# A decoder trunk on one core: column sums of five modulation groups as transposes spread over four weight items, and a new order of VectorE's work in the GLA output projection

## The chip, the cores and the metric

The kernel runs on one core of a Trainium2 chip. The metric is the device time of one execution in microseconds (us), lower is better. An execution with the hardware profiler gives the trace that is read here.

## The reference, cut to what matters

One token block of 256 rows (T) by 2048 columns (D) goes through a gated-linear-attention (GLA) layer with a convolutional gated MLP, then a latent-attention (MLA) layer with another MLP. Each block is modulated by vectors computed from a condition vector c:

```python
c_act = jax.nn.silu(c)
mod = c_act @ mod_w[i] + mod_b[i]            # 1 x 2048 times 2048 x 12288
sh_m, sc_m, g_m, sh_f, sc_f, g_f = jnp.split(mod, 6, axis=-1)
h = modulate(rmsnorm(x, norm_mix_g[i]), sh_m, sc_m)
y = gla_mixer(h, ...)                        # its last step: o @ w_o, 256x2048 times 2048x2048
x = x + (1 + g_m)[:, None, :] * y
h = modulate(rmsnorm(x, norm_ffn_g[i]), sh_f, sc_f)
x = x + (1 + g_f)[:, None, :] * conv_ffn(h, ...)
```

## The kernel before, in words

**Weight items.** Every large product streams its weights in items of 128x2048 floats (1 MB; 0.75 MB in the last part of each MLP), 16 to a 2048x2048 matrix. An item passes four stages: SyncE (SP) starts the load into `raw`, ScalarE copies it to a rounded high part (`hi`, L756), VectorE subtracts to get the low part (`lo`, L1202), and TensorE multiplies: 16 matmuls with the high part, then 8 with the low part (L1868, L1869, L1875; in items with transposes between the products L1860 to L1862). There are RAW = 4 slots, so the load of item n waits until TensorE has finished item n-4, and the helpers of ScalarE and VectorE work AHEAD = 3 items before TensorE: at step k of a section VectorE makes the low part of item k+3.

**Modulation groups.** The 14 vectors g = 0 to 13 (2048 wide) are sums of 16 tiles each, `mod_w` rows times a column of c. A modulation step (L1219) is one load of 1 MB into one of MODS = 2 buffers (L550) and one VectorE operation, `acc += mods * c`. Its load waits until the step two before it is done (L548). MOD_PLACES (L437) says at which item's step the modulation steps are done; on SP's queue the load of a step at item k stands right ahead of the load of item k+3 (L626), and on VectorE the step stands ahead of the low part of item k+3.

**Column sums.** When a group is complete, `acc` must be summed over its 128 partitions. For the gates (2, 5, 11, 13) TensorE does four wide products with a matrix of ones (L1940). For shifts and scales it does 16 one-column products with the tile as stationary matrix (L1945) in one block, and one or two tiny VectorE operations finish (`reduced`, L1230): group 3 after item 14 of the section `r`, 6 and 8 after the third item of `up01` and `up02`, 7 and 9 after the third item of `down01` and `down02`.

**GLA output.** Section `r` (16 items) ends with the output of head 3 (`head_out`). Section `gla_out` then multiplies the gated heads by `w_o`. Its left operand is made on the way: TensorE transposes `r_sb` by pairs of tiles (`turn_head`, L1909, 8 fills), ScalarE and VectorE split each fill into `h_hi` (L771) and `h_lo` (L1274, L1281), and the first four items wait for them fill by fill. VectorE's order at the end of `r` and in the first steps (L1577 to L1594, L1339 to L1352):

```python
if k == 15: reduced(3); o_split_lo(0); o_split_lo(1)
mods_at(s.item + k); lo(s.item + AHEAD + k)   # the last: item 2 of gla_out
...
gated_head(3)                                 # then, per step k of gla_out:
if k < 3: o_split_lo(2*k+2); o_split_lo(2*k+3)
if k == 7: add_chunk(1)
mods_at(k); lo(AHEAD + k)
if k in (3, 11): add_chunk(k // 4)            # add_last after the loop
```

`add_chunk` (L1304, L1305) adds a finished chunk of four items to x; `add_last` (L1311 to L1316) adds the last one in two halves, and the norm that follows waits for it.

Of the kernel before, what the change touches and what calls it, by code (L numbers as in the profile page):

```python
# [29 lines left out]
P = 128  # L30
# [19 lines left out]
def sections():  # L50
# [11 lines left out]
        ("r", 1, 16, 4, 0, 0),  # L62
        ("o", 1, 0, 0, 8, 6),
        ("mod_r", 1, 0, 0, 0, 1),
        ("o3", 1, 0, 0, 0, 2),
        ("gla_out", 2, 8, 2, 0, 0),
# [10 lines left out]

    ffn(0, (4, 1, 1), (1, 1, 1))
    s += [
# [58 lines left out]
def yoco_kernel(nc, x, c, positions, mod_w, mod_b, norm_mix_g, norm_ffn_g, gla_w_in, gla_w_gate2,  # L138
# [155 lines left out]

    GATES = (2, 5, 11, 13)

    REDUCE = {0: ("pre", 10), 1: ("pre", 11), 2: ("mod_v", 0), 3: ("mod_r", 0), 4: ("mod_gla", 0),
# [6 lines left out]
    def fills_of(g):  # L304
        return 4 if g in GATES else 1

# [4 lines left out]
    with ExitStack() as ctx:  # L311
# [120 lines left out]
        def taken(m):  # L432
# [6 lines left out]
            ("r", 3, 3, every[:13]), ("r", 4, 0, (13, 13, 14, 15)),  # L439
            ("gla_out", 4, 4, (4, 4, 5, 5, 6, 7, 8, 9, 10, 11, 12, 13)),  # L440
            ("up00", 5, 0, (3, 4, 5, 6, 6, 7) + after_conv[:10]), ("up00", 6, 0, after_conv[10:]),
# [68 lines left out]
        def o_fill(h, t):  # L510
            return (at["o"].ms + 2 * h if h < 3 else at["o3"].ms) + t

# [231 lines left out]
        def _(act):  # L744
# [221 lines left out]
            head_squares(3)  # L966
            hi(s.item + AHEAD + 15)

            def add_section(name, after):

                s = a[name]
                for k in range(16):
                    if k < 3:
                        o_split_hi(2 * k + 2)
                        o_split_hi(2 * k + 3)
# [216 lines left out]
        def _(dve):  # L1192
# [28 lines left out]
            def gate_row(g, j):  # L1221
# [6 lines left out]
                dve.scalar_tensor_tensor(v, ms[:, fill % 2, :], 1.0, v, ALU.add, ALU.add).then_inc(ms_free, 1)  # L1228

            def reduced(g):  # L1230

# [104 lines left out]
            def add_section(name, after):  # L1336

                s = a[name]
                for k in range(15):  # L1339
                    if k < 3:  # L1340
                        o_split_lo(2 * k + 2)
                        o_split_lo(2 * k + 3)
                    if k == 7:
                        add_chunk(s.chunk + 1, 1, slice(W, 2 * W))
                    mods_at(s.item + k)
                    if k < 14:
                        lo(s.item + AHEAD + k)
                    if k in (3, 11):
                        ch = k // 4
                        add_chunk(s.chunk + ch, ch % 2, slice(ch * W, (ch + 1) * W))  # L1350
                add_last(name, after)
                lo(s.item + AHEAD + 14)  # L1352
# [225 lines left out]
            for k in range(16):  # L1578
                score_step(16 + k)
                if 3 <= k < 7:  # L1580
                    gate_row(2, k - 3)
                if k in (8, 11, 14):
                    gated_head((8, 11, 14).index(k))
                if k == 15:
                    reduced(3)
                    o_split_lo(0)
                    o_split_lo(1)
                mods_at(s.item + k)
                lo(s.item + AHEAD + k)
# [45 lines left out]
            def up(layer, g, before=None):  # L1635
# [5 lines left out]
                def body(i, conv_too):  # L1641
                    for k in range(8):
                        mods_at(s.item + 8 * i + k)
# [7 lines left out]
                        if before is not None and not conv_too and k == 2:  # L1651

                            reduced(before)
                        if conv_too and 1 <= k <= 4:
                            conv_lo(i - 1, k - 1, tile_ - 1)
# [5 lines left out]
            def down(layer, g, up_group):  # L1661
# [15 lines left out]
                for k in range(16):  # L1677
# [7 lines left out]
                    if k == 15:  # L1685

                        add_chunk(s.chunk + 3, 1, slice(3 * W, 4 * W))
                    mods_at(s.item + k)
# [4 lines left out]
                    if up_group in GATES:  # L1693

                        if 3 <= k < 7:
                            gate_row(up_group, k - 3)
                        if k == 6:
                            dve.wait_ge(ms_free, reduce_at(up_group) + 4)
                            add_chunk(s.chunk, 0, slice(0, W))
                    elif k == 2 and up_group is not None:  # L1700
                        reduced(up_group)
                    if k % 4 == 3 and k < 15 and not (k == 3 and up_group in GATES):
# [144 lines left out]
        def _(pe):  # L1847
# [84 lines left out]
            def reduce_mod(g, parts=range(4)):  # L1932
# [9 lines left out]
                else:  # L1942
# [4 lines left out]
                    ins.then_inc(ms_done, 1)  # L1947

            def turn_rows(name, fills, tile_of):

# [30 lines left out]
            def section(name, hi_s, lo_s, turned=None):  # L1981
# [198 lines left out]
            for k in range(16):  # L2180
# [11 lines left out]
                if k == 13:  # L2192
                    turn_head(0)
                    turn_head(1)
                if k == 14:
                    reduce_mod(3)
            head_out(3)
# [10 lines left out]
            def ffn(layer, norm, up_groups, down_groups):  # L2208
                for g, blocks in enumerate(UP_BLOCKS):
                    s = a[f"up{layer}{g}"]  # L2210

                    def block_(i, turn):
                        for k in range(8):
# [17 lines left out]
                    for k in range(16):  # L2231
# [7 lines left out]
                        if k < 2:  # L2239
# [3 lines left out]
                            turn_pair(layer, g, blocks - 1, 2 * k + 1)  # L2243
                        if up_groups[g] in GATES:
                            if 2 <= k < 6:
                                reduce_mod(up_groups[g], (k - 2,))
                        elif k == 2 and up_groups[g] is not None:
                            reduce_mod(up_groups[g])

# [169 lines left out]
```

## Time and profile before

| | |
|---|---|
| median of 3 runs | 2425.52 us (2422.24 to 2425.59) |
| the profiled execution | 2417.79 us, of which its span 2416.0 us |
| granted TensorE clock, mean | 0.981 |
| busy: TensorE, VectorE, ScalarE, GpSimd | 96%, 76%, 45%, 5% of the span |
| one-column products L1945 | 128 products in 8 blocks |
| section gla_out, items 0 to 15 | 434.40 to 533.83 us |

In timelines a row gives start and duration in us, engine, line, operation, `out<-in` and tile; the bracket is the idle time just before and what ended it. Matmul rows overlap: what a matmul costs is the distance to the next start, not its duration.

### The profile page before, as it was taken

What the parts mean: (1) busy time and instruction counts of PE and PEld (TensorE: products, weight loads), DVE (VectorE), ACT (ScalarE), POOL (GpSimd) and SP (SyncE); (2) the same over time, 40 slices, a digit from 0 to 9 for tenths busy, and PEclk for the clock granted to TensorE, in tenths of its full rate; (3) what the DMA queues carried; (4) which work ended last, traced back from release to release, by engine and by line L of the source; (5) the groups of instructions that cost most, each with busy time, mean ns of one, the idle gap of its engine ahead of it and who ended that gap; (6) DMA issues with size and microseconds to landing.
All of it is one profiled execution on the core that took longest, in us unless ns stands there. A gap on an engine that the chain in (4) does not pass through costs nothing.

```text
span 2416.0 us, 26990 instructions
## 1 busy us (share of the span) xinstructions
PE 2326.8 (96%) x10880; PEld 1883.1 (78%) x10880; DVE 1835.2 (76%) x1728; ACT 1097.7 (45%) x1192; POOL 126.8 (5%) x145
## 2 busy tenths in 40 slices
PE   5999999989999999999999999999999999999998
PEld 2478887778887888888877788777887888878876
DVE  5868997787998888888888777787786555654565
ACT  2244434344544345533454555434654345543553
POOL 0022730000000000000000000000000000000000
PEclk8999999999999999999999999999999999999999
DMA  9958689587987988789878465785775555555544
GB/s 362 378 199 300 248 313 355 203 316 274 346 326 274 367 312 308 279 334 363 306 253 326 131 223 196 271 320 211 277 283 203 191 188 180 189 174 192 188 164 152
DMA packets 259808, 632.91 MB, mean 262 GB/s; under 512 B 23505, under 2 KB 32745, under 8 KB 233978
## 3 DMA queue, kind: packets, MB, share of 16 engines
q1 hardware_dynamic: 258050, 625.90, 72.6%
q10 hardware_dynamic: 1656, 5.60, 0.6%
q8 instruction: 70, 1.15, 0.2%
q14 instruction: 32, 0.26, 0.0%
HBM read 629.36 MB, written 2.10 MB: 261 GB/s over the span
## 4 chain that ended last, share of the span: by engine, by line
PE 81%; DVE 8%; DMA 5%; ACT 3%; issue 2%; SPq 1%; POOL 1%; DVEq 0%; POOLq 0%; ACTq 0%
PE gm L1868 22%; PE gm L1869 22%; PE gm L1875 21%; PE tp L1909 2%; DMA raw<-in_ffn_w_down_dram 2%; PE gm L1860 2%; PE gm L1862 2%; PE gm L1861 2%; DVE w_lo L1202 2%; ACT w_hi L756 2%; DVE acc L1219 1%; DVE conv L1609 1%; DMA raw<-in_gla_w_o_dram 1%; PE ms L2007 1%; DMA mods<-in_mod_w_dram 1%
## 5 line engine op out<-in xcount | busy, mean ns | idle before, releaser
L1202 DVE TENSOR_TENSOR w_lo<-raw,w_hi 128x2048 fp32r<-128x2048 f32 (+1 forms) x378 | 851.8, 2256 | 350.5 <-ACT w_hi L756 349.0
L756 ACT ACTIVATE w_hi<-raw 128x2048 fp32r<-128x2048 f32 (+1 forms) x378 | 703.9, 1863 | 709.0 <-DMA raw<-in_ffn_w_up_dram 240.0
L1868 PE MATMUL gm<-w_hi,h_hi 128*128 128x512 f32 x1816 | 722.0, 398 | 1.9 <-DVE h_lo L1281 1.6
L1869 PE MATMUL gm<-w_hi,h_lo 128*128 128x512 f32 x1816 | 709.7, 391 | 0.0
L1875 PE MATMUL gm<-w_lo,h_hi 128*128 128x512 f32 x1816 | 448.8, 389 | 0.0
L1219 DVE SCALAR_TENSOR_TENSOR acc<-mods,c_col,acc 128x2048 f32<-128x2048 f32 x180 | 423.0, 2350 | 6.2 <-DMA mods<-in_mod_w_dram 5.8
L1868 PEld LDWEIGHTS gm<-w_hi,h_hi 128*128 128x128 f32 x1816 | 342.3, 189 | 80.4 <-issue 6.3
L1869 PEld LDWEIGHTS gm<-w_hi,h_lo 128*128 128x128 f32 x1816 | 342.4, 189 | 70.3 <-issue 1.7
L1875 PEld LDWEIGHTS gm<-w_lo,h_hi 128*128 128x128 f32 x1816 | 340.8, 188 | 71.0 <-DVE w_lo L1202 0.2
L1868 PE MATMUL gm<-w_hi,a_hi 128*128 128x512 f32 x692 | 279.6, 404 | 10.8 <-DVE a_lo L1632 8.8
L1869 PE MATMUL gm<-w_hi,a_lo 128*128 128x512 f32 x692 | 274.7, 397 | 0.0
L1609 DVE SCALAR_TENSOR_TENSOR conv<-tp,cv_col,conv 128x255 f32<-128x255 f32 (+1 forms) x352 | 152.4, 478 | 86.2 <-ACT conv L1018 82.8
L1875 PE MATMUL gm<-w_lo,a_hi 128*128 128x512 f32 x692 | 172.2, 389 | 0.0
L1868 PEld LDWEIGHTS gm<-w_hi,a_hi 128*128 128x128 f32 x692 | 133.3, 193 | 44.3 <-DVE a_lo L1632 11.9
L1869 PEld LDWEIGHTS gm<-w_hi,a_lo 128*128 128x128 f32 x692 | 133.3, 193 | 28.9 <-issue 1.4
L1875 PEld LDWEIGHTS gm<-w_lo,a_hi 128*128 128x128 f32 x692 | 129.9, 188 | 27.0
L762 ACT ACTIVATE u<-gm 128x1024 f32<-128x1024 f32 x76 | 77.5, 1020 | 147.0 <-PE gm L1875 142.8
L1018 ACT ACTIVATE conv<-tp,cv_col 128x256 f32<-128x256 f32 x176 | 88.3, 560 | 117.4 <-PE tp L1909 116.9
L694 POOL TENSOR_TENSOR sq<-sq 128x2 f32<-128x2 f32 x4 | 4.9, 1220 | 1856.1 <-ACT tp L788 1856.1
L725 POOL TENSOR_TENSOR ex<-ex,qk_t 128x512 f32<-128x512 f32 x32 | 78.8, 2480 | 105.3 <-ACT ex L929 105.3
L771 ACT ACTIVATE h_hi<-tp,ab 128x256 fp32r<-128x256 f32 x64 | 32.0, 563 | 84.2 <-DVE ab L1402 47.8
L1860 PE MATMUL gm<-w_hi,h_hi 128*128 128x512 f32 x136 | 58.1, 427 | 8.7 <-DVE h_lo L1281 5.3
(261 smaller groups left out, 2129.7 us busy)
## 6 DMA issues: line engine op xcount, KB each, us to landing
raw<-in_ffn_w_up_dram SPq DMA_DIRECT2D x176, 1024.0 KB, 5.1
mods<-in_mod_w_dram SPq DMA_DIRECT2D x170, 1024.0 KB, 7.1
raw<-in_ffn_w_down_dram SPq DMA_DIRECT2D x64, 1024.0 KB, 5.1
raw<-in_gla_w_in_dram SPq DMA_DIRECT2D x48, 1024.0 KB, 5.2
mods<-in_kv_mod_w_dram SPq DMA_DIRECT2D x32, 1024.0 KB, 6.9
raw<-in_ffn_w_down_dram SPq DMA_DIRECT2D x32, 768.0 KB, 4.4
raw<-in_gla_w_o_dram SPq DMA_DIRECT2D x16, 1024.0 KB, 7.4
raw<-in_mla_w_o_dram SPq DMA_DIRECT2D x16, 1024.0 KB, 5.3
```

The lines of the kernel that those rows point to most:

```text
L725: pool.tensor_tensor(f, f, s, ALU.mult).then_inc(xq_made, 1)
L756: act.activation(w_hi[:, k % RAW, 0:words], raw[:, k % RAW, 0:words], ACT.Copy).then_inc(hi_made, 1)
L762: act.activation(dst, gm[:, par] if src is None else src, func).then_inc(u_made, 1)
L1018: ins = act.activation(conv[:, j % 2, side, :], tp[:, bank, side * T:(side + 1) * T], ACT.Identity, scale=cv_col[:, layer, 2, cs], bias=cv ...
L1202: dve.tensor_tensor(w_lo[:, k % RAW, 0:words], raw[:, k % RAW, 0:words], w_hi[:, k % RAW, 0:words].bitcast(F32), ALU.subtract).then_inc(lo ...
L1219: return dve.scalar_tensor_tensor(total, tile_, ck, total, ALU.mult, ALU.add)
L1609: ins = dve.scalar_tensor_tensor(v, tp[:, bank, side * T:(side + 1) * T - shift], cv_col[:, layer, tap, cs], v, ALU.mult, ALU.add)
L1860: pe.matmul(o, hi_s[:, kt, tok], wh[:, j, :], start=kt == 0, stop=False)
L1861: pe.matmul(o, hi_s[:, kt, tok], wl[:, j, :], start=False, stop=False)
L1868: pe.matmul(o, hi_s[:, kt, tok], wh[:, j, :], start=kt == 0, stop=False)
L1869: pe.matmul(o, lo_s[:, kt, tok], wh[:, j, :], start=False, stop=False)
L1875: return pe.matmul(o, hi_s[:, kt, tok], wl[:, j, :], start=False, stop=kt == total - 1)
```

## The change

Groups 3, 6, 7, 8 and 9 (TURNED) get four fills in place of one: after each of four consecutive items TensorE does four transposes of `acc` into a bank of `ms`, and VectorE sums each bank along its rows (`row_sums`, 128x512 to 128x4), then adds the bias. Group 3 moves from the end of `r` to the steps after items 4 to 7 of `gla_out`. In the MLPs this work, and that of the gates, stands ahead of the modulation steps and the low part of its step. In `gla_out` VectorE does four low splits ahead of `gated_head(3)`, the low part of an item ahead of the modulation steps and adds of its step, and the modulation step of `r`'s last item comes after the low part of item 3. One modulation step moves from item 5 to item 4 and one from 4 to 3. ScalarE does the high splits of a pair ahead of the high part of the item.

```diff
-        ("o", 1, 0, 0, 8, 6), ("mod_r", 1, 0, 0, 0, 1), ("o3", 1, 0, 0, 0, 2),
+        ("o", 1, 0, 0, 8, 8), ("mod_r", 1, 0, 0, 0, 4),
...
-    ffn(0, (4, 1, 1), (1, 1, 1))
+    ffn(0, (4, 4, 4), (4, 4, 1))
...
+    TURNED = (3, 6, 7, 8, 9)
...
-            ("gla_out", 4, 4, (4, 4, 5, 5, 6, 7, 8, 9, 10, 11, 12, 13)),
+            ("gla_out", 4, 4, (3, 4, 4, 5, 6, 7, 8, 9, 10, 11, 12, 13)),
...   ScalarE, end of r
-            hi(s.item + AHEAD + 15)
+            for k in range(3):
+                o_split_hi(2 * k + 2)
+                o_split_hi(2 * k + 3)
+                hi(s.item + AHEAD + 15 + k)
...   VectorE
+            def row_sums(g, j):
+                fill = reduce_at(g) + j
+                dve.wait_ge(ms_done, made(fill))
+                dve.reduce_sum(modc[:, 1, 4 * j:4 * j + 4],
+                               ms[:, fill % 2, :].rearrange("p (b k) -> p b k", b=4), AX_X).then_inc(ms_free, 1)
...   VectorE, add_section of gla_out
-                for k in range(15):
-                    if k < 3:
-                        o_split_lo(2 * k + 2)
-                        o_split_lo(2 * k + 3)
-                    if k == 7:
-                        add_chunk(s.chunk + 1, 1, slice(W, 2 * W))
-                    mods_at(s.item + k)
+                for k in range(2, 15):
+                    if 5 <= k < 9:
+                        row_step(3, k - 2)
                     if k < 14:
                         lo(s.item + AHEAD + k)
-                    if k in (3, 11):
+                    if k in (3, 7, 11):
                         ch = k // 4
                         add_chunk(s.chunk + ch, ch % 2, slice(ch * W, (ch + 1) * W))
+                    mods_at(s.item + k)
...   VectorE, end of r
-                if k == 15:
-                    reduced(3)
-                    o_split_lo(0)
-                    o_split_lo(1)
-                mods_at(s.item + k)
-                lo(s.item + AHEAD + k)
+                if k < 15:
+                    mods_at(s.item + k)
+                    lo(s.item + AHEAD + k)
...
+            for f in range(4):
+                o_split_lo(f)
             gated_head(3)
+            lo(s.item + AHEAD + 15)
+            o_split_lo(4)
+            o_split_lo(5)
+            lo(s.item + AHEAD + 16)
+            mods_at(s.item + 15)
+            o_split_lo(6)
+            o_split_lo(7)
+            lo(s.item + AHEAD + 17)
...   TensorE
+            def reduce_turned(g, part):
+                pe.wait_ge(mod_used, KT * (g - 1))
+                fill = reduce_at(g) + part
+                o = ms_open(fill)
+                for b in range(4):
+                    c0 = part * W + b * P
+                    ins = pe.transpose(o[:, b * P:(b + 1) * P], acc[:, g % 2, c0:c0 + P], ident[:, :])
+                ins.then_inc(ms_done, 1)
...   TensorE, first body of gla_out
+                        if turned and k >= 4:
+                            reduce_turned(3, k - 4)
...   TensorE, up and down
-                            if g and not turn and k == 2 and down_groups[g - 1] is not None:
-                                reduce_mod(down_groups[g - 1])
+                            if g and not turn and 2 <= k < 6 and down_groups[g - 1] is not None:
+                                reduce_turned(down_groups[g - 1], k - 2)
```

## Rows read from the trace of the kernel before

**Rows 1.** The page: busy time and share of the span of each engine

```profile
PE 2326.8 (96%) x10880; PEld 1883.1 (78%) x10880; DVE 1835.2 (76%) x1728; ACT 1097.7 (45%) x1192; POOL 126.8 (5%) x145
```

**Rows 2.** Windows: us, busy PE, PEld, DVE, ACT, POOL, granted clock, DMA share, GB/s

```profile
434.00:484.00 50.00, 47.23 (x218) 38.32 (x217) 40.05 (x38) 20.36 (x26) 3.31 (x2) 1.00 0.61 230
484.00:534.00 50.00, 46.50 (x195) 36.98 (x195) 44.31 (x23) 23.17 (x25) 2.20 (x2) 0.97 0.93 355
1287.00:1330.00 43.00, 37.25 (x164) 29.68 (x162) 37.47 (x25) 18.82 (x22) 1.27 (x2) 0.96 0.93 350
```

**Rows 3.** Timeline of TensorE: end of `r`, item 4 and item 15 of gla_out

```profile
420.75 3.70 PE L1945 MATMUL ms<-ones,acc 128*128 128x1 f32 x32 [0.36 <-DVE r_sb L1571]
424.32 0.48 PE L1868 MATMUL gm<-w_hi,h_hi 128*128 128x512 f32 x1
...
461.80 0.39 PE L1868 MATMUL gm<-w_hi,h_hi 128*128 128x512 f32 x1
462.03 0.39 PE L1869 MATMUL gm<-w_hi,h_lo 128*128 128x512 f32 x1
...
526.61 0.50 PE L1860 MATMUL gm<-w_hi,h_hi 128*128 128x512 f32 x1 [3.43 <-DVE w_lo L1202]
```

**Rows 4.** Timeline of TensorE: between 435.61 and 436.51 four transposes; a wait at 443

```profile
435.61 0.39 PE L1862 MATMUL gm<-w_hi,h_lo 128*128 128x512 f32 x1
...
436.20 0.48 PE L1860 MATMUL gm<-w_hi,h_hi 128*128 128x512 f32 x1
436.51 0.40 PE L1861 MATMUL gm<-w_lo,h_hi 128*128 128x512 f32 x1
...
443.45 0.47 PE L1860 MATMUL gm<-w_hi,h_hi 128*128 128x512 f32 x1 [2.40 <-DVE h_lo L1281]
```

**Rows 5.** Groups by shape: the one-column products, and a read of one bank of `ms`

```profile
L1945 PE MATMUL ms<-ones,acc 128*128 128x1 f32 x256 | 29.4, 249 | 0.4 <-DVE r_sb L1571 0.4
...
L1228 DVE SCALAR_TENSOR_TENSOR gate_b<-ms,gate_b 128x512 f32<-128x512 f32 x16 | 11.0, 685 | 0.0
```

**Rows 6.** Windows of 10 us from a block's start (groups 3, 6, 8), and one with transposes

```profile
420.70:430.70 10.00, 9.95 (x53) 8.69 (x54) 5.11 (x4) 1.59 (x1) 0.00 (x0) 0.83 0.36 125
840.20:850.20 10.00, 10.00 (x61) 8.85 (x61) 8.55 (x5) 2.55 (x2) 0.00 (x0) 1.00 1.01 390
...
1118.60:1128.60 10.00, 10.00 (x55) 8.83 (x54) 8.64 (x5) 2.67 (x3) 0.00 (x0) 0.83 1.03 392
...
589.00:601.00 12.00, 12.00 (x56) 9.93 (x55) 7.82 (x4) 4.65 (x4) 0.00 (x0) 1.00 0.91 337
```

**Rows 7.** Timeline of VectorE: steps 3 to 5 of gla_out, and the last add

```profile
464.86 2.29 DVE L1202 TENSOR_TENSOR w_lo<-raw,w_hi 128x2048 fp32r<-128x2048 f32 x1 [4.67 <-ACT w_hi L756]
467.07 1.22 DVE L1304 TENSOR_TENSOR u<-u,gate_b 128x1024 f32<-128x1024 f32 x1
...
469.47 4.80 DVE L1219 SCALAR_TENSOR_TENSOR acc<-mods,c_col,acc 128x2048 f32<-128x2048 f32 x2
474.18 2.29 DVE L1202 TENSOR_TENSOR w_lo<-raw,w_hi 128x2048 fp32r<-128x2048 f32 x1
...
531.03 0.69 DVE L1311 TENSOR_TENSOR u<-gm,gate_b 128x512 f32<-128x512 f32 x1
```

**Rows 8.** Timeline of SP's queue: a modulation step's load, then that of item 12

```profile
496.52 0.33 SPq L550 DMA_DIRECT2D mods<-in_mod_w_dram  x1
496.90 0.43 SPq L540 DMA_DIRECT2D raw<-in_gla_w_o_dram  x1
```

**Rows 9.** Timeline of ScalarE: the high parts of items 8 and 12

```profile
481.88 1.92 ACT L756 ACTIVATE w_hi<-raw 128x2048 fp32r<-128x2048 f32 x1 [9.47 <-DMA raw<-in_gla_w_o_dram]
...
504.03 1.92 ACT L756 ACTIVATE w_hi<-raw 128x2048 fp32r<-128x2048 f32 x1 [3.40 <-DMA raw<-in_gla_w_o_dram]
```

**Rows 10.** The page's DMA issues: KB each, median us from issue to landing

```profile
raw<-in_gla_w_in_dram SPq DMA_DIRECT2D x48, 1024.0 KB, 5.2
```

**Rows 11.** DMA issues between 484 and 534 us, same columns

```profile
raw<-in_gla_w_o_dram SPq DMA_DIRECT2D x5, 1024.0 KB, 9.6
```

More of the change, by code:

```diff
@@ L62, in sections @@
         ("r", 1, 16, 4, 0, 0),
-        ("o", 1, 0, 0, 8, 6),
-        ("mod_r", 1, 0, 0, 0, 1),
-        ("o3", 1, 0, 0, 0, 2),
+        ("o", 1, 0, 0, 8, 8),
+        ("mod_r", 1, 0, 0, 0, 4),
         ("gla_out", 2, 8, 2, 0, 0),
@@ L304, in fills_of @@
     def fills_of(g):
-        return 4 if g in GATES else 1
+        return 4 if g in GATES or g in TURNED else 1
     def reduce_at(g):
@@ L510, in o_fill @@
         def o_fill(h, t):
-            return (at["o"].ms + 2 * h if h < 3 else at["o3"].ms) + t
+            return at["o"].ms + 2 * h + t
         UNIT_STEP = (0, 1) + tuple(n + 1 for n in range(2, len(UNITS)))
@@ L966, in _ @@
             head_squares(3)
-            hi(s.item + AHEAD + 15)
+            for k in range(3):
+                o_split_hi(2 * k + 2)
+                o_split_hi(2 * k + 3)
+                hi(s.item + AHEAD + 15 + k)
             def add_section(name, after):
                 s = a[name]
-                for k in range(16):
-                    if k < 3:
-                        o_split_hi(2 * k + 2)
-                        o_split_hi(2 * k + 3)
+                for k in range(2, 16):
                     if k % 4 == 3 and k < 15:
@@ L1228, in gate_row, with turned_columns, row_step @@
                 dve.scalar_tensor_tensor(v, ms[:, fill % 2, :], 1.0, v, ALU.add, ALU.add).then_inc(ms_free, 1)
+            def row_sums(g, j):
[3 more added lines that the diff above has]
+                               ms[:, fill % 2, :].rearrange("p (b k) -> p b k", b=4), AX_X).then_inc(ms_free, 1)
+            def turned_columns(g):
+                dve.wait_ge(ms_free, reduce_at(g) + 4)
+                tile_, col = mod_bias(g)
+                bias = pcol[:, tile_, col:col + KT]
+                if g in SHIFT:
+                    step.link(dve.tensor_tensor(ab[:, A_OF[SHIFT[g][0]] + 1, :], modc[:, 1, :], bias, ALU.add))
+                else:
+                    norm, gain = SCALE[g]
+                    step.link(dve.tensor_tensor(modc[:, 0, :], modc[:, 1, :], bias, ALU.add))
+                    dve.scalar_tensor_tensor(ab[:, A_OF[norm], :], modc[:, 0, :], 1.0,
+                                             pcol[:, 0, gain:gain + KT], ALU.add,
+                                             ALU.mult).then_inc(columns_on, 1)
+                    dve.wait_ge(columns_on, list(SCALE).index(g) + 1)
+            def row_step(g, k):
+                if 3 <= k < 7:
+                    if g in GATES:
+                        gate_row(g, k - 3)
+                    else:
+                        row_sums(g, k - 3)
+                if k == 6:
+                    if g in GATES:
+                        dve.wait_ge(ms_free, reduce_at(g) + 4)
+                    else:
+                        turned_columns(g)
             def reduced(g):
@@ L1338, in add_section @@
                 s = a[name]
-                for k in range(15):
-                    if k < 3:
-                        o_split_lo(2 * k + 2)
-                        o_split_lo(2 * k + 3)
-                    if k == 7:
-                        add_chunk(s.chunk + 1, 1, slice(W, 2 * W))
-                    mods_at(s.item + k)
+                for k in range(2, 15):
+                    if 5 <= k < 9:
+                        row_step(3, k - 2)
                     if k < 14:
                         lo(s.item + AHEAD + k)
-                    if k in (3, 11):
+                    if k in (3, 7, 11):
                         ch = k // 4
                         add_chunk(s.chunk + ch, ch % 2, slice(ch * W, (ch + 1) * W))
+                    mods_at(s.item + k)
                 add_last(name, after)
@@ L1642, in body @@
                     for k in range(8):
+                        if before is not None and not conv_too:
+                            row_step(before, k)
                         mods_at(s.item + 8 * i + k)
@@ L1650, in body @@
                             lo(s.item + AHEAD + 8 * i + k)
-                        if before is not None and not conv_too and k == 2:
-                            reduced(before)
                         if conv_too and 1 <= k <= 4:
@@ L1687, in down @@
                         add_chunk(s.chunk + 3, 1, slice(3 * W, 4 * W))
+                    if up_group is not None:
+                        row_step(up_group, k)
                     mods_at(s.item + k)
@@ L1692, in down @@
                         last_tiles(0)
[L1693 to L1701, printed above, removed]
+                    if up_group in GATES and k == 6:
+                        add_chunk(s.chunk, 0, slice(0, W))
                     if k % 4 == 3 and k < 15 and not (k == 3 and up_group in GATES):
@@ L2194, in _ @@
                     turn_head(1)
-                if k == 14:
-                    reduce_mod(3)
             head_out(3)
@@ L2243, in ffn @@
                             turn_pair(layer, g, blocks - 1, 2 * k + 1)
-                        if up_groups[g] in GATES:
-                            if 2 <= k < 6:
+                        if up_groups[g] is not None and 2 <= k < 6:
+                            if up_groups[g] in GATES:
                                 reduce_mod(up_groups[g], (k - 2,))
-                        elif k == 2 and up_groups[g] is not None:
-                            reduce_mod(up_groups[g])
+                            else:
+                                reduce_turned(up_groups[g], k - 2)
             ffn(0, "norm1", (5, 7, 9), (6, 8, 10))
```

## The prediction

> **What bounds the kernel now.** I read the page first: TensorE is busy 96% of the span [rows 1], so time saved on TensorE counts wherever nothing else sets the pace, and anything that makes it wait costs. Then I read the windows, because that share is an average. In the first half of the GLA output section the transfer engines are busy 0.61 of the time, in the second 0.93 at 355 GB/s, with VectorE busy 44.3 of 50 us [rows 2]. An item costs TensorE 24 products at a pitch of 0.23 [rows 3], 5.4 us, and in the second half every item comes with one modulation step, so 2 MB must land in that time: TensorE lives there from hand to mouth. The timelines confirm it. The high part of item 8 is only started at 481.88 [rows 9], although TensorE had reached item 4 at 461.80 and needs item 8 four items later, at about 483.6; the section ends with a wait of 3.43 for the last low part [rows 3]. Two more things show ahead of that section: a block of one-column products of 3.57 (420.75 to 424.32) after a wait of 0.36 [rows 3], and a wait of 2.40 for `h_lo` [rows 4].
>
> **Part 1, the column sums in the MLPs (groups 6 to 9).** Eight blocks take 29.4 us busy together, 3.7 each; the start-to-start distance of group 3's is 3.57 [rows 3, 5], and I take 3.6. Four transposes between products: from 435.61 to 436.51 is 0.90, less two pitches of 0.23 is 0.44 [rows 4], so four groups cost 1.8. Saved 1.8 per group, 7.2 for four. The clock adds to it: in the 10 us from group 8's block the mean granted clock is 0.83, so TensorE stood at 1.2 GHz for a third of it; four such windows stand at 0.83, those of groups 3, 7, 8 and 9 (two are shown), and only group 6's at 1.00 [rows 6]. At most 10 x 0.17 = 1.7 is lost in each; part of the low stretch lies on the block itself, so I take 1.4. If nothing fell any more, that is 4.2 for three groups; the bounds are 0 and 5.1. A stretch with four transposes between items, as the change makes them, stands at 1.00 [rows 6]. VectorE gets four sums of 128x512 per group. The nearest row reads such a bank in 0.685 [rows 5]; 2.7 us per group, spread over four steps. At group 6 VectorE is busy 8.55 of 10 [rows 6], one step of 5.4 becomes 0.7 longer, and its parts are made three items ahead: I cost it at nothing. In `down02` it is not free: VectorE is busy 37.5 of 43 [rows 2] and the last items are starved, so 1.0 of the gain goes back there (bounds 0 and 2.7). The sums and gate rows now ahead of the low part wait for TensorE's fill one item back, which is done when VectorE, three items ahead in the weights but held by their loads, gets there; nothing. The loads at groups 6 and 8 run at 390 GB/s: 2.1 MB in 5.4 us, just TensorE's pace, so the gain stays. Part 1: 7.2 + 4.2 - 1.0 = 10.4, in round numbers **10.5 us faster** (6 to 13).
>
> **Part 2, the start of the GLA output.** The block goes (3.57 + 0.36), with it the low clock behind it (0.83 [rows 6], 1.7 us). The wait of 2.40 goes as well: the splits of fills 2 and 3 no longer stand behind a modulation step, a low part and the gating of head 3. What is late next: the splits of fills 6 and 7, which now stand behind the modulation step of `r`'s last item (2.35, as one in rows 7). I take 1.3 of it, bounds 0 and 2.35. So item 4 starts 3.57 + 0.36 + 1.7 + 2.4 - 1.3 = 6.7 earlier, at 455.1. The four transposes cost 1.8 afterwards.
>
> **Part 3, low parts ahead of modulation steps: the decisive one.** The load of the step at k goes to SP right ahead of the load of item k+3 and waits until the step two before it has been done. Before, VectorE did that step ahead of the low part of item k+1; so a load hung on the low part three items back. Now the step stands behind the low part of its row, and a load hangs on the low part **two** items back. One turn of that ring: from the issue of item 12's load (496.90) to its high part (504.03) 7.1 [rows 8, 9], high part 1.9, low part 2.2, modulation step 2.35 [rows 7], and 0.4 from the step's issue to the item's (496.52 to 496.90) [rows 8]. That is 14.0 for two items, 7.0 each, against TensorE's 5.4; by three items, as before, it was 4.7 and hidden. In steps 3, 7 and 11 an add of 2.4 (467.07 to 469.47 [rows 7]) now stands in the ring too.
>
> Laid out: item 3 ends at 455.1; the low part of item 6 starts 3.06 later (461.80 to 464.86 [rows 3, 7]) and ends at 460.4, the add at 462.8, the first step at 465.2. Only then can SP issue the third step and item 7 (465.6); it lands at 472.7, its low part ends at 476.9, the second step at 479.2, and item 8 goes out at 479.6. Its high part ends at 488.6 instead of 483.8 [rows 9]. Then every 14.0, with an add twice: item 10 at 493.6, 12 at 510.0, 14 at 524.0, 16 (the first of `up00`) at 540.4. Item 16 lands at 547.5, its low part ends at 551.7, and the last modulation step at 554.1. Behind them in VectorE's order stands the first half of the last add, at 531.03 before [rows 7], and behind that the norm and all that follows. **23 us later**, with Part 2 and the 1.8 inside, since all of it lies before the ring. The row sums of group 3 stand in the ring's steps 5 to 8 and make TensorE wait for a bank at items 6 and 7, where it would wait for weights anyway: nothing more. The wait itself will drop the clock; that falls into waiting time as well.
>
> The one price that is uncertain is the landing. Alone it is 5.2 [rows 10], in the saturated stretch 9.6 [rows 11]; the ring runs the transfer engines at three quarters, one step and one item at a time, which is item 12's case (7.1). Five turns are priced with it: 23 - 5 x 1.9 = 13.5 at the low end, 23 + 5 x 2.5 = 35.5 at the high end, where the high end would need full transfer engines and so is hardly reached.
>
> **Sum.** Against the profiled execution, 2417.8: + 23 - 10.5 = 2430.3. It stands 7.7 below the median of the runs, 2425.5; on that the forecast is **2438.0 us**, 12.5 slower (0.5%). A measurement of this kernel can tell some 0.2%, 4.9 us, from no change.
>
> **Rivals.**
> - **The ring doesn't bind (faster).** The saturated stretch before was paced by the transfer engines (0.93 busy, 9.6 to land), not by order; were VectorE far enough ahead for the new order to cost only waiting that is there anyway, the section would keep Part 2's 6.7, less 1.8, and get back some 2 of the 3.4 at item 15: 7, with Part 1's 10.5 together 17.5, 2408. Against: the low part can't be done before its item lands, and VectorE waited 4.67 for one already at step 3 [rows 7]. Chance 0.17.
> - **Short landings (no change).** With the transfer engines free between turns an item lands near 5.2, and the ring costs 13.5: + 3, 2428.5. For: the engines idle a quarter. Against: two transfers go out together each time. With what lies around it chance 0.12.
> - **Transposes don't hold the clock (slower still).** TensorE's clock would fall after each group of four, and the 4.2 of Part 1 would not come: 2442. Chance 0.10. The Trainium skill, TensorE: Matmul & The Clock Gate, Part 4: PE-mode transpose, says that a transpose doesn't count as work for the clock; by that rule alone groups of transposes would lower it. The trace disagrees where they stand between items, at 1.00 [rows 6].
> - The forecast itself: 0.61, own range 2429 to 2450.
>
> The change does more than its name says: five groups are turned, not one. Left out of it, Part 1 would be nothing and the time 2448; it is in the diff, so I give that no chance.
>
> **Chances and range.** Faster by over 0.2%: 0.17, the first rival. Within: 0.12. Slower: 0.61 + 0.10 = 0.71. The range 2416 to 2451 takes in the forecast with its landing bounds, the second and third rival and the near side of the first; left out are most of the 0.17 below and a little above.
>
> **What would show it.** Right: the high part of `gla_out`'s item 8 ends near 488.6 and the last add's first half starts near 554; TensorE waits 3 to 9 us several times between items 7 and 15; the loads L550 in that section wait for L1219, and the transfer engines stand near 0.75; TensorE reaches item 4 at 455; L1945 shrinks to three blocks (3, 6, 7, 8, 9 gone); no low clock at 1026, 1118 and 1261. Wrong: items at 5.5 us through the section; or a low clock still behind the transposes; or the row sums near 1.4 us each, which would starve `down02`.

## The result and the profile after

The changed kernel takes 2438.6 us (median of six runs, 2435.35 to 2445.4), the kernel before in the same comparison 2425.56 (six runs, 2422.24 to 2427.34): 1.006 times as long, with a 95% interval from 1.0043 to 1.0076. It is slower, by 13.0 us between the medians (14.6 by the ratio) where 12.5 were forecast. The profiled execution of after has a span of 2435.0 us at a mean granted clock of 0.978.

The page's busy times, then the windows that answer to [rows 2] with one more between them (columns as there):

```profile
PE 2320.7 (95%) x10800; PEld 1877.1 (77%) x10800; DVE 1847.2 (76%) x1748; ACT 1098.2 (45%) x1192; POOL 125.0 (5%) x145
```

```profile
434.00:484.00 50.00, 39.06 (x180) 31.55 (x180) 34.73 (x30) 16.15 (x17) 0.00 (x0) 0.93 0.48 173
484.00:534.00 50.00, 42.88 (x174) 34.27 (x173) 32.48 (x19) 17.68 (x17) 0.00 (x0) 0.93 0.79 295
534.00:560.00 26.00, 17.92 (x73) 14.99 (x71) 19.89 (x13) 10.21 (x12) 5.25 (x5) 0.79 0.63 232
1287.00:1330.00 43.00, 42.34 (x187) 33.77 (x185) 36.02 (x25) 16.40 (x19) 0.00 (x0) 1.00 0.94 346
```

TensorE's busy total hardly moved, and that alone would hide the matter. Both windows of the GLA output show it: TensorE is busy 39.1 and 42.9 us of 50 where it was 47.2 and 46.5 [rows 2], and in the second one VectorE fell from 44.3 to 32.5 us and the transfer engines from 0.93 to 0.79. All three have room, and none of them is full: that is what a ring of waits looks like. SyncE's queue shows who holds it. Its waits from 430 to 560 us (in total, times, longest) in after:

```profile
SPq L550 <- DVE acc L1219: 83.3, 10, 15.7
SPq L540 <- PE gm L1895: 28.1, 4, 8.9
```

In before the loads of the items (L540) mostly wait for TensorE to free a slot, and the loads of the steps (L550) wait little more than half as long (in total, times, longest):

```profile
SPq L540 <- PE gm L1862: 62.1, 7, 18.0
SPq L550 <- DVE acc L1219: 46.5, 10, 9.4
SPq L540 <- PE gm L1875: 17.0, 3, 10.9
```

The queue's timeline in after. The rows of L540 are the loads of items 7, 8, 10, 12, 14 and 16:

```profile
465.56 0.43 SPq L540 DMA_DIRECT2D raw<-in_gla_w_o_dram  x1
479.18 0.33 SPq L550 DMA_DIRECT2D mods<-in_mod_w_dram  x1
479.55 0.43 SPq L540 DMA_DIRECT2D raw<-in_gla_w_o_dram  x1
...
493.64 0.43 SPq L540 DMA_DIRECT2D raw<-in_gla_w_o_dram  x1
...
510.14 0.43 SPq L540 DMA_DIRECT2D raw<-in_gla_w_o_dram  x1
...
524.16 0.43 SPq L540 DMA_DIRECT2D raw<-in_gla_w_o_dram  x1
...
540.53 1.86 SPq L540 DMA_DIRECT2D raw<-in_ffn_w_up_dram  x3
```

And one turn as VectorE sees it (timeline; the bracket is the wait ahead): a low part, two modulation steps and a row sum, then nothing to do for 6.48 us, the next low part.

```profile
474.59 2.29 DVE L1202 TENSOR_TENSOR w_lo<-raw,w_hi 128x2048 fp32r<-128x2048 f32 x1 [9.45 <-ACT w_hi L756]
476.80 4.80 DVE L1219 SCALAR_TENSOR_TENSOR acc<-mods,c_col,acc 128x2048 f32<-128x2048 f32 x2
481.52 0.68 DVE L1234 TENSOR_REDUCE modc<-ms 128x4 f32<-128x512 f32 x1
488.69 2.29 DVE L1202 TENSOR_TENSOR w_lo<-raw,w_hi 128x2048 fp32r<-128x2048 f32 x1 [6.48 <-ACT w_hi L756]
```

TensorE's waits in the section, in order of time:

```profile
482.35 1.09 PE L1989 MATMUL ms<-ident,acc 128*128 128x128 f32 x4 [9.77 <-DVE modc L1234]
...
493.99 0.63 PE L1989 MATMUL ms<-ident,acc 128*128 128x128 f32 x4 [3.04 <-DVE modc L1234]
...
519.32 0.47 PE L1901 MATMUL gm<-w_hi,h_hi 128*128 128x512 f32 x1 [1.33 <-ACT w_hi L756]
...
533.20 0.50 PE L1901 MATMUL gm<-w_hi,h_hi 128*128 128x512 f32 x1 [2.74 <-ACT w_hi L756]
...
542.38 0.80 PE L1893 MATMUL gm<-w_hi,h_hi 128*128 128x512 f32 x1 [3.43 <-DVE w_lo L1202]
...
554.35 1.86 PE L1978 MATMUL ms<-ones,acc 128*128 128x1 f32 x8 [4.65 <-DVE acc L1219]
...
566.22 0.79 PE L1893 MATMUL gm<-w_hi,h_hi 128*128 128x512 f32 x1 [1.35 <-DVE h_lo L1316]
```

The row at 554.35 is the block of group 4, which waits for the last modulation step. The last row is the first item of `up00`. In the trace of before it stands 22.9 us earlier:

```profile
543.32 0.80 PE L1860 MATMUL gm<-w_hi,h_hi 128*128 128x512 f32 x1 [1.36 <-DVE h_lo L1281]
```

### The profile page after: what moved, and what is told of

The parts are those of the page before. It is cut to its first block, busy times and chain, and to the rows that moved or that the text cites. A ratio compares the mean times of both kernels' runs of the same rounds, so it can differ in the third digit from the quotient of the medians.

```text
span 2435.0 us, 26862 instructions
## 1 busy us (share of the span) xinstructions
PE 2320.7 (95%) x10800; PEld 1877.1 (77%) x10800; DVE 1847.2 (76%) x1748; ACT 1098.2 (45%) x1192; POOL 125.0 (5%) x145
## 4 chain that ended last, share of the span: by engine, by line
PE 78%; DVE 9%; DMA 6%; ACT 3%; issue 2%; SPq 1%; POOL 0%; DVEq 0%; POOLq 0%; ACTq 0%
PE gm L1901 21%; PE gm L1902 21%; PE gm L1908 21%; PE tp L1942 2%; DMA raw<-in_ffn_w_down_dram 2%; ACT w_hi L756 2%; DVE w_lo L1202 2%; DVE acc L1219 2%; PE gm L1893 2%; PE gm L1895 2%; PE gm L1894 2%; DVE conv L1648 1%; DMA raw<-in_gla_w_o_dram 1%; PE ms L2052 1%; PE ms L2186 1%
## 5 line engine op out<-in xcount | busy, mean ns | idle before, releaser
L1219 DVE SCALAR_TENSOR_TENSOR acc<-mods,c_col,acc 128x2048 f32<-128x2048 f32 x180 | 422.6, 2348 | 7.0 <-DMA mods<-in_mod_w_dram 5.9
```

What stands on the lines that cost most here:

```text
L1219: return dve.scalar_tensor_tensor(total, tile_, ck, total, ALU.mult, ALU.add)
```

## The experiments

Each kernel was timed in turn with the kernel before on one chip; ratios are to that. The sets ran on three chips, so kernels of different sets are compared by their ratios. The first four share one set of runs of before (median 2423.66 of 17), the next four another (2425.5 of 17), the last two a third (2423.82 of 7).

**1. After, with the modulation steps ahead of the low part again.**

```diff
     in add_section of gla_out, for k in range(2, 15):
+                    mods_at(s.item + k)
                     if k < 14:
                         lo(s.item + AHEAD + k)
...
-                    mods_at(s.item + k)
```

> The changed kernel with one edit: in the GLA output section VectorE does the modulation steps of a step ahead of its low part again; all else stays. The ring theory: a load hangs on the low part three items back again, 4.7 us per item, so the transfers (some 5.4 per item and step) set the pace. Item 8's load goes out near 465 to 466 instead of 479.6, that of item 16 near 511 instead of 540.5, the wait of TensorE for a bank of the row sums is gone or under 2 us, and the section gives back some 30 us or more: 2404 to 2410, 15 to 21 below the kernel before. Rival, the row sums of group 3 are what stops TensorE (it waits 9.8 and 3.0 for them in the trace of the changed kernel): they stay where they are, so the time stays within 5 us of the changed kernel's 2438.6.

Measured: 2402.32 us (2399.48 to 2406.2), ratio 0.9911 [0.989, 0.9932]. One line moved back, past the low part and in steps 3, 7 and 11 past the add, turns 13 us slower into 21 us faster, a little more than was expected. SyncE issues item 7 at 458.99, item 8 at 466.27 and item 16 at 508.08, where after had 465.56, 479.55 and 540.53:

```profile
458.99 0.43 SPq L540 DMA_DIRECT2D raw<-in_gla_w_o_dram  x1
...
466.27 0.66 SPq L540 DMA_DIRECT2D raw<-in_gla_w_o_dram  x1
...
508.08 4.69 SPq L540 DMA_DIRECT2D raw<-in_ffn_w_up_dram  x2
```

The transposes of group 3 stand in the same four places and now wait for nothing, and the wait for the last low part is down to 0.27.

**2. After, with only SyncE's order changed:** in `gla_out` the load of an item goes out ahead of the load of the modulation step. VectorE's order is that of after.

```diff
-                for m in mod_at.get(n - AHEAD, ()):
+                late = a["gla_out"].item <= n - AHEAD < a["gla_out"].item + 16
+                for m in () if late else mod_at.get(n - AHEAD, ()):
                     load_mod(*m)
...
                 load_item(n, src)
+                for m in mod_at.get(n - AHEAD, ()) if late else ():
+                    load_mod(*m)
```

> The changed kernel with one edit: in the GLA output section SP issues the load of an item ahead of the modulation load of its step, where the changed kernel has it behind; VectorE's new order stays. The ring theory says that the new order costs only because an item's load stands behind a modulation load that waits for a step; with the queue turned an item's load hangs on the step one further back, so again three items, and it lands some 2.5 earlier: 2404 to 2412, close to the kernel with the old order. Rival, the new order is bad in itself (VectorE waits with the low part for the high part and does its steps too late, so the steps pile up): then this kernel stays near 2438.6, at least 2430.

Measured: 2404.84 us (2401.11 to 2407.41), ratio 0.9922 [0.9901, 0.9943], on a par with the first. The ring needs both of its halves: VectorE's step behind a low part that waits for its load, and a load behind the load of a step. Breaking either frees the section; so what cost the time was neither the order on VectorE nor the order on SyncE, but the two together.

**3. Before, with only the new order of low part, adds and modulation steps.** No group is turned, no split is dealt early.

```diff
     in add_section of gla_out, for k in range(15):
-                    if k == 7:
-                        add_chunk(s.chunk + 1, 1, slice(W, 2 * W))
-                    mods_at(s.item + k)
                     if k < 14:
                         lo(s.item + AHEAD + k)
-                    if k in (3, 11):
+                    if k in (3, 7, 11):
                         ...
+                    mods_at(s.item + k)
```

> The kernel before with one edit: in the GLA output section the low part, and the add, stand ahead of the modulation steps of their step; no transposed sums, no other order at the end of r. The ring theory: the ring of two items holds from item 8 to item 16, four turns of 14 with the adds of steps 3, 7 and 11 in it, so item 8's load near 478, item 12's near 515, item 16's near 546, and the norm some 30 later: 2448 to 2460, slower than both kernels. Rival, the loss in the changed kernel comes from its early start meeting loads that can't follow, or from the row sums: then this one costs under 10 us, 2426 to 2435.

Measured: 2454.84 us (2450.24 to 2458.23), ratio 1.0127 [1.0104, 1.015], 31 us slower than before. This prices the ring alone. The loads of items 8, 12 and 16 went out at 486.93, 522.70 and 553.34, 7 to 9 us later than expected; 5.2 of it is TensorE reaching `gla_out` later than in before's trace (439.56 against 434.40). In its windows the transfer engines drop to 0.41 and 0.70 and TensorE's clock to 0.84 in the second:

```profile
434.00:484.00 50.00, 47.45 (x208) 37.60 (x207) 34.16 (x36) 20.52 (x28) 3.31 (x2) 0.97 0.41 148
484.00:534.00 50.00, 35.75 (x130) 27.89 (x129) 27.55 (x14) 12.92 (x14) 0.00 (x0) 0.84 0.70 261
```

**4. Before, with only groups 6 to 9 turned,** and the order of the GLA output as it was (TURNED = (6, 7, 8, 9); group 3 stays a block at the end of `r`; the gate rows of the MLPs stand where the change has them).

> The kernel before with the transposed sums of groups 6 to 9 alone (and the gate rows where the change has them); the GLA output as before. By the prediction's first part 10.5 us faster, 2415. By what the trace of the changed kernel shows, less: group 7's block hid a wait for a_lo that now shows with 2.3, and down02 takes its gain back, so 5 to 8 us: 2417.5 to 2420.5. Rival, that the transposes and row sums bring nothing in the whole (the clock falls at another place instead, supply bound stretches absorb the rest): 2423 to 2428.

Measured: 2417.5 us (2413.43 to 2423.31, 12 runs), ratio 0.9977 [0.9963, 0.9991]: 5.6 us faster by the ratio, 2 to 9 by its interval. Less than the 10.5 of Part 1; where it went is in the section on the prediction.

**5 and 6. Parts of the first experiment undone:** group 7 alone as a block again, then groups 6 to 9 all as blocks (TURNED = (3, 6, 8, 9), and TURNED = (3,)).

> The kernel of e1_mods_first with group 7 alone summed by the block of one-column products again, after item 2 of down01. Theory: that block (3.6) hid a wait of item 3 for a_lo, which ends some 2.9 after item 2, and with the transposes 2.3 of it shows as a wait; so turning group 7 gained 0.8 plus at most 1.4 of clock, not 3.2. Here TensorE shows no wait for a_lo at item 3, and the stretch from item 2's start to item 6's start of down01 is 0.8 longer (27.1 against 26.3 in the changed kernel) if the clock falls behind the block as in the kernel before, and shorter than there if it doesn't. The whole time stays within 2 us of e1_mods_first's 2402. Rival, the prediction's price: the stretch grows by 3.2 and the time by 3.

> The kernel of e1_mods_first with groups 6 to 9 summed by blocks of one-column products again: the early start of the GLA output and the turned group 3 alone. If the parts add up, it lies 21.3 less 6.2 = 15 below the kernel before (e1_mods_first less what e4_turned gained alone): 2408 to 2410. Of these, 7 to 8 come from the section up to item 4 and the end of it as the schedule had it, the rest from item 15's wait and the norm. Rival, the MLP part gains more when the trunk arrives earlier, or its low clocks fall elsewhere: 2412 or more, or under 2404.

Measured: 2402.45 us (2397.8 to 2407.88), ratio 0.9906 [0.988, 0.9932] for the fifth, and 2410.78 (2406.47 to 2414.83), 0.9943 [0.9924, 0.9963] for the sixth. Turning group 7 back changes nothing in the time that these runs can tell. TensorE shows no wait for `a_lo` there, as expected, but the stretch from item 2 to item 6 of `down01` takes 28.69 where 27.1 was expected, with a granted clock of 0.66 in the 10 us from the block's start. The sixth against before is the GLA output without the ring: 13.8 us faster (0.0057 x 2425.5); with the four groups' 5.6 that is 19.4, and the first experiment gave 0.0089 x 2424 = 21.6. The two parts add, within the intervals.

**7. The first, with two modulation steps one item earlier.**

```diff
-            ("gla_out", 4, 4, (3, 4, 4, 5, 6, 7, 8, 9, 10, 11, 12, 13)),
+            ("gla_out", 4, 4, (2, 3, 4, 5, 6, 7, 8, 9, 10, 11, 12, 13)),
```

> The kernel of e1_mods_first with the modulation steps of the GLA output at items 2, 3, 4, ... 13, one each, in place of 3, 4, 4, 5, ... 13: the first load goes out one item earlier and no step is doubled. By the ring by three, item 8 and the last low part come 1 to 2 earlier and the time is 1 to 3 below e1_mods_first: 2399 to 2402. Rival, from item 8 on the transfer engines set the pace and the end of the section is TensorE's own in e1_mods_first (its wait at item 15 is down to 0.27), so that nothing is left to gain: within 1 us of it.

Measured: 2401.07 us (2398.03 to 2401.96), ratio 0.9899 [0.9877, 0.9921]. The gain over the first, 1.2 us by the medians and 2.9 by the ratios, is inside the intervals.

**8. The first, with the row sums and gate rows of the MLPs behind the low part of their step,** as one would place work that nobody seems to wait for.

```diff
-                        if before is not None and not conv_too:
-                            row_step(before, k)
                         ...   the low part
+                        if before is not None and not conv_too:
+                            row_step(before, k)
     the same for row_step(up_group, k)
```

> The kernel of e1_mods_first with the row sums and gate rows of the MLPs behind the low part of their step, where the gate rows stood before. Theory: VectorE is three items ahead there and the sums cost nothing in either place but for down02, where the loads are late at the end: 0 to 1 faster, 2401 to 2403. Rival, that the sums ahead of the low part hold up the chain of loads and steps in down02 (its items start 1.6 later at item 14 in the changed kernel than its item 4 would allow): 2 to 3 faster, below 2400.

Measured: 2413.82 us (2409.14 to 2421.95, 12 runs), ratio 0.9954 [0.994, 0.9969]: 10.4 slower than the first by the ratios, 11.5 by the medians, where I had expected no loss. A miss, and the most useful one. `ms` has two banks: the transposes of the third step need the bank that the row sum of the first gives back. TensorE's waits for a row sum between 800 and 1330 us, and one of them in the timelines of TensorE and VectorE:

```profile
PE ms L1989 <- DVE modc L1234: 10.4, 5, 3.8
```

```profile
847.99 1.09 PE L1989 MATMUL ms<-ident,acc 128*128 128x128 f32 x4 [3.82 <-DVE modc L1234]
```

```profile
844.95 2.29 DVE L1202 TENSOR_TENSOR w_lo<-raw,w_hi 128x2048 fp32r<-128x2048 f32 x1 [0.91 <-ACT w_hi L756]
847.15 0.68 DVE L1234 TENSOR_REDUCE modc<-ms 128x4 f32<-128x512 f32 x1
```

The row sum of 0.68 us stands behind a low part, which waits for a high part, which waits for a load; TensorE, which runs in order, waits for the bank and with it for that load, three items ahead of its own need. Five such waits come to 10.4 us, which is the loss; in the first experiment there is none. The 9.77 and 3.04 in after's GLA output are the same wait: there the row sum stands behind a low part and the modulation steps after it.

**9. The first, with group 9 alone as a block.**

> The kernel of e1_mods_first with group 9 summed again in one block of 16 one-column products after down02's third item. Stretch read: from the second group of four convolution transposes ahead of down02's item 2 to the first transposes of the norm behind down02; with group 9 turned it took 79.5 (after), 78.5 (e1), 78.0 (e4) and 77.9 (e5), with the block 79.5 (before) and 78.8 (e6). My theory: the supply of weights sets that stretch, so the block's 1.9 us are made up before the last item: 78 to 79.5, and the time is e1's within 1 us, with the block followed by a low clock. Rival: TensorE paces down02, the stretch grows to 80.5 or more, and the time is 2 us longer than e1's.

Measured: 2407.12 us (2400.93 to 2408.93, 4 runs), ratio 0.9926 [0.9905, 0.9948]. The stretch in question runs from 1241.85 to 1322.02, 80.2 us, between what the theory and its rival asked for, and the time is 3.6 us above the first's by the ratios (4.8 by the medians); the intervals of the ratios overlap. That leans to the rival, but is inconclusive by itself. All profiled executions together have 79.5, 80.6, 78.8 and 80.2 with the block (before and experiments 3, 6, 9; mean 79.8), and 79.5, 78.5, 78.7, 78.0, 77.9, 78.7, 78.0 and 77.3 turned (after and experiments 1, 2, 4, 5, 7, 8, 10; mean 78.3). So `down02` keeps about 1.4 us of what group 9 gives: my theory, that supply sets the whole stretch, was too strong, and so was the rival. The clock behind the block is the one expected (window of 10 us from its start):

```profile
1248.70:1258.70 10.00, 10.00 (x54) 8.67 (x54) 5.02 (x8) 2.63 (x5) 0.00 (x0) 0.83 0.52 185
```

**10. The seventh with the second's order on SyncE:** both cures at once.

> The kernel of e7_places (modulation steps ahead of the low parts, at items 2, 3, 4, ... of gla_out) with e2_items_first's order on SyncE (each item's load ahead of the modulation step's, in gla_out). The two each break the ring by themselves. My theory: the ring is gone already in e7, so the second cure adds nothing: e7's time within 2 us, 2399 to 2403, item 15's wait under 1, the first of up00 at e7's place within 1 us. First rival: item 12 to 15 are still late by the order on the queue, and the time falls by another 2 to 4 us. Second rival: with VectorE's step ahead of the low part and its load now behind the item's, VectorE waits for the step's data and the low parts come late again: 3 to 10 us slower than e7.

Measured: 2400.58 us (2398.69 to 2403.55), ratio 0.9906 [0.9889, 0.9924]: the seventh's time within 0.5 us by the medians, and 1.7 above it by the ratios, inside the intervals. The ring was gone already, and the second cure adds nothing to the first.

## Why the prediction was right, point by point

**Part 3, the ring, was right in its steps.** It asked for the loads of items 7, 8, 10, 12, 14 and 16 at 465.6, 479.6, 493.6, 510.0, 524.0 and 540.4; they went out at 465.56, 479.55, 493.64, 510.14, 524.16 and 540.53. The high part of item 8, foreseen to end at 488.6, ran from 486.75 for 1.91, to 488.66. The first half of the last add, foreseen behind 554.1, started at 554.21, and the first item of `up00` is 22.9 later than in before's trace, for 23 (on what that trace is worth, see the offset below). The price that I had called uncertain, the landing, is that of item 12: the median of the section is 7.1.

```profile
raw<-in_gla_w_o_dram SPq DMA_DIRECT2D x16, 1024.0 KB, 7.1
```

With that the rivals of an order that doesn't bind and of short landings fall for this kernel. The first of them described what the section would be without the ring, and put its price at 7 us with Part 2. Experiment 1 is that kernel: the first item of `up00` starts at 533.11, 10.2 earlier than in before's trace, and experiment 6, which has before's column sums in the MLPs, is 13.8 faster in its times. So that rival's price was 3 to 7 too small. Experiment 3, the new order without Part 2, should by the same working cost 23 + 6.7 - 1.8 = 27.9; it cost 31, with an interval from 25 to 36.

The other signs asked for came too: the loads L550 wait for L1219, the transfer engines stand at 0.79 in the second window, the one-column products of L1945 are down from 256 records to 96 (three blocks; two records are one product), and a row sum takes 0.68, like the read in [rows 5]. Of the waits of 3 to 9 us on TensorE, 9.77, 3.04 and 3.43 came; 1.33 and 2.74 were shorter.

**Part 2 was right where it can be read:** item 4 started at 455.14, for 455.1. The wait of 2.40 for a low split shrank to 1.08, and item 3 started at 449.60. Over more executions it gained more, as the paragraph on the offset shows.

**Part 1 was mis-sized: 5.6 us by experiment 4, forecast 10.5** (6 to 13). Its terms, read from item 2's start to item 6's in the section of each group: group 6 from 25.39 to 23.58, 1.8 saved as forecast. Group 8 from 26.95 to 23.57, 3.4 for 3.2. Group 7 from 27.08 to 26.28, 0.8 for 3.2. Group 9: 1.9 saved over those four items, and by item 15 of `down02` nothing left in this pair, 1.4 over all executions, for 2.2. With 1.4 for group 9 that is 7.4 for 10.4, inside experiment 4's interval (2 to 9). Two steps failed.

The step for group 7 took the block's whole time as TensorE's. In fact it was cover. Before, the block ran from 1026.37 to 1030.00, and meanwhile ScalarE and VectorE finished the left operand of the next item; now that item waits for it. The operand's last part in before, then TensorE in after:

```profile
1028.48 0.76 DVE L1632 TENSOR_TENSOR a_lo<-gated,a_hi 128x256 fp32r<-128x256 f32 x2
```

```profile
1049.23 0.60 PE L1989 MATMUL ms<-ident,acc 128*128 128x128 f32 x4
...
1052.17 0.50 PE L1901 MATMUL gm<-w_hi,a_hi 128*128 128x512 f32 x1 [2.34 <-DVE a_lo L1671]
```

I had asked of each new piece of work what hides it, and not of the removed block what it had hidden. Over the executions the stretch takes 27.1 with the block (before, experiments 3 and 6) and 28.7 in experiment 5. Turned it takes 26.3 to 26.5 (after, experiments 1, 4 and 7) but 27.9 to 28.2 in experiments 2, 9 and 10, where the clock was low behind the wait. The means are 27.5 and 27.0, so turning group 7 gained even less than the 0.8 of this pair, and experiment 5's time shows no difference at all.

The step for group 9 took 1.0 off for the starved end of `down02`, by the four row sums on VectorE; it should have been nearly 2. The likely reason, which experiment 9 leaves open, is that the end is set by the supply of weights (transfer engines at 0.94 and 346 GB/s from 1287 us on), which TensorE only reaches sooner.

**The clock, and the third rival.** Windows of 10 us in after, from the first transposes of groups 7 and 8, and one from 774 us:

```profile
1049.20:1059.20 10.00, 7.66 (x38) 6.18 (x37) 7.74 (x11) 4.22 (x6) 0.00 (x0) 1.00 0.59 214
1140.80:1150.80 10.00, 10.00 (x49) 8.34 (x48) 8.38 (x5) 2.65 (x3) 0.00 (x0) 1.00 1.03 410
```

```profile
774.00:784.00 10.00, 10.00 (x37) 7.68 (x36) 4.70 (x4) 3.51 (x3) 0.00 (x0) 0.83 0.55 207
```

In after the clock stays at its upper level behind both groups. The other executions tell it less simply. The 10 us from group 7's first transposes in experiment 2:

```profile
1015.76:1025.76 10.00, 7.67 (x29) 6.03 (x28) 7.70 (x11) 2.97 (x4) 0.00 (x0) 0.83 0.55 210
```

I leave experiment 8 with its waits aside. Where TensorE goes straight on after the transposes, at groups 6 and 8, the clock is low behind the first of them in none of eight executions. At group 7, where the wait of 2.3 to 2.6 for `a_lo` follows, it is low in three of seven (experiments 2, 9 and 10), and at group 9 in one of seven (experiment 5). The blocks were followed by the lower level at groups 3, 7 and 8 in every execution that has them, at group 9 in three of four, at group 6 in none of three. So the third rival, by which the clock falls behind every group of transposes, is not what happens here. But a part of it is true: of the 1.4 that I had put on the clock for each of groups 7, 8 and 9, group 8's is safe, and group 7's comes in some executions only.

The Trainium skill (TensorE: Matmul & The Clock Gate, Part 4: PE-mode transpose) says that a transpose does not count as work for the clock. By that rule alone groups of transposes would lower it; behind four transposes after an item of 24 products, at groups 6 and 8, they did not. At group 9's place in after the clock is low, 0.75 in the 10 us from 1274.6, but ahead of the first transpose at 1281.17.

**The offset.** Between the two profiled executions the spans differ by 19.0 us, between the medians by 13.0: before's profiled execution was 7.8 below its median, after's 1.8. It had been quick in places that have nothing to do with the change, and two of them can be named.

The first is the end of `r`, on which Part 2 was priced. From item 14 of `r` to item 4 of `gla_out` TensorE took 47.1 us in before's trace, but 49.7 and 50.3 in experiments 3 and 4, which have before's order there. The wait ahead of group 3's block alone is 0.36 in before and these in the other two:

```profile
425.93 3.70 PE L1943 MATMUL ms<-ones,acc 128*128 128x1 f32 x32 [1.37 <-DVE r_sb L1569]
```

```profile
423.10 4.31 PE L1975 MATMUL ms<-ones,acc 128*128 128x1 f32 x32 [1.99 <-DVE r_sb L1607]
```

After and the experiments with its new start take 40.2 to 40.7. So Part 2 gained 6.9 against before's profiled execution and 9 to 10 against the two others. The 22.9 of Part 3 carries the same error: against experiment 4, whose GLA output is before's, the first item of `up00` comes only 18.3 later (566.22 against 547.97). The times agree. After and experiment 4 differ in Parts 2 and 3 alone, and by their ratios (1.006 and 0.9977) that is 20 us, with both intervals 15 to 25.

The second is `down00`. Its items 0 to 3 took 27.8 to 28.1 us in before and in experiments 2 and 5 to 10, and 30.2 to 30.9 in after and in experiments 1, 3 and 4. In after and experiment 1 a stretch at the lower clock came in (the window from 774 us above), in experiment 3 longer waits for a tile of the convolution (1.87 and 0.97 where before has 0.54) at a full clock, in experiment 4 both. Experiments 1 and 5 have the same instructions up to there, and so have before and experiment 4, and each pair is split. At the same place in before:

```profile
750.30:760.30 10.00, 9.93 (x42) 7.86 (x43) 5.72 (x4) 4.19 (x3) 0.00 (x0) 1.00 0.71 273
```

So the forecast's 12.5 is a difference of two terms that were both on the large side: 23, where the times give some 20 with 23 inside the interval, and 10.5, where they give 5.6 with 10.5 outside it. That only 0.5 us is left against the medians is luck; the chain of waits was foreseen step by step, the two sizes less well.

## What to carry to other kernels

Where a load waits for a consumer's buffer, everything behind it on the same issuing queue waits too; so count, on the consumer's engine, how many items back the operation that frees the buffer stands, and price one turn (landing, conversions, the operation) against that many items of the pace. A swap of two lines on VectorE took one item off that distance, three to two, and cost 36 us against experiment 1. Work that gives back a shared bank belongs ahead of anything that waits for a load, however short it is. And before a block is credited in full for its removal, ask which wait it was covering.

## What was not expected

- The placement of a 0.68 us row sum behind the low part cost 10.4 us (experiment 8), through a bank two transposes later.
- The start of `down00` took some 2.4 us longer in four of twelve executions, by a low clock, by waits or by both, with the same instructions ahead of it or not; the end of `r` with the first items of `gla_out` took 2.6 to 3.2 us longer in two executions with before's order than in before's own. So a single trace can be 2 to 3 us off at one place for no cause in the kernel.
- Group 8's gain includes the clock (3.4 where the work is 1.8), group 6's doesn't: of the blocks of one-column products some are followed by the lower level and some are not, and no run here tells what decides it. This wasn't tried further.

The version of experiment 7 beats both kernels: 2401.07 us, 0.9899 of before.
